# A hybrid decoder step: the meetings between head groups moved, group A's state stores and sample products spread out

## The chip, the core and the metric

The kernel runs on one core of one Trainium2 chip. The core has five engines that run their own instruction streams and meet only through semaphores: TensorE (PE, matrix products; PEld is its weight load), VectorE (DVE), ScalarE (ACT), GpSimd (POOL) and SyncE (SP, which here only issues DMA transfers). The metric is the device time of one execution in microseconds (us); lower is better.

## The reference

Two layers of a decoder trunk. Each layer normalises its input, projects it with `w_in`, runs four head groups side by side, gates and concatenates them, and projects back with `w_out`. There are 512 prompt tokens and 8 sample sequences of 4 new tokens each. The change touches group A, retention, and what stands between the groups.

```python
h = _rmsnorm(x, g)
p = _split_cols(jnp.einsum('nld,dc->nlc', h, w_in))
ret_o, ret_s = _retention(...)        # A
sb_o = _stick_breaking(...)           # B
dsa_o = _dsa(...)                     # C
rw_o, wkv_s = _rwkv7(...)             # D
x = x + jnp.einsum('nlc,cd->nld', mix, w_out)

def step(S, inp):                     # retention, one chunk
    qc, kc, vc = inp
    att = jnp.einsum('nqhd,nkhd->nhqk', qc, kc) * dmask[None]
    o = (jnp.einsum('nhqk,nkhe->nqhe', att, vc)
         + jnp.einsum('nqhd,nhde->nqhe', qc, S) * q_dec[None, :, :, None])
    S = S * s_dec[None, :, None, None] + jnp.einsum('nkhd,nkhe->nhde', kc * k_dec[None, :, :, None], vc)
    return S, o
```

For the samples each of the 8 sequences has its own state S per head (4 heads, 64 x 128). The new states are results and have to be stored (`p_ret` for the prompt, `s_ret` for the samples).

## The kernel before, in words

**The stream.** In each layer the projection by `w_in` is the bulk of the work. It is cut in 62 tiles of 128 output columns; a tile in 4 pieces (a piece is 128 x 4 x 128 weights, one DMA of 256 KB issued by SP at L336), a piece in 4 units. A unit is 6 matrix products of 128 x 272 (L319). Each piece is cast by ACT (L345, `in_w_hi`), its rest is made by DVE (L349, `in_w_lo`), and PE may use it then. Four parted pieces and three raw ones fit on the chip: the load of piece u waits until piece u-3 is parted, the cast of u until PE is done with u-4.

**The mixers beside it.** The four head groups (classes Retention, StickBreaking, Sparse, TokenMix, here A to D) run beside the stream on the same engines. Each has one generator per engine. The generator for PE says after each of its steps how many units of the stream come next (`yield 4` is four units, some 3 us). Each such yield is a mark. `Beside.follow` runs the generators of the other engines in step with those marks: at each mark they do their piece of the mixer, and then what the stream needs of them at that point. `yield n` on those engines passes n marks over; `yield LAST` passes all that are left. The four mixers start at stream unit 64, 320, 576 and 864; between the end of one and the start of the next PE runs the stream alone.

**The meetings.** The mixers share the four banks `bank`, the buffers and some semaphores, so no engine may begin the next mixer before all five have ended the last. Before, this is `meet`, called as the last thing in each of the 20 generators:

```python
def meet(engine, left, n):
    engine.drain().then_inc(left, 1)
    engine.wait_ge(left, 5 * n)
```

The engine waits until its own work is done, counts up the semaphore `left`, and waits until all five have done so.

**Group A's end.** For the samples PE computes scores (L1129), the products with the values (L1136), and then, for 4 heads and 8 sequences, the product of the old state with the 4 query columns of that sequence (L1139: 32 products, weights 128 x 128, 4 columns moving). A product in f32 is shown by the profile as two records, so L1139 has 64 records in each layer. Only heads 2j and 2j+1 share a weight `state_s[:, s, j, :]` (they lie in the upper and lower 64 rows; `qdz` holds the queries with the other half zero). Then PE gives 4 units, and for each head it makes the growth of the sample states (L1150), which DVE adds (L1259, semaphore `advanced`), with 4 units between. Norm sums (L1160) and a `yield 3` close the group.

SP loads the old states at A's start, and passes over all marks of A. After the last one it does this:

```python
yield LAST
sp.wait_ge(self.carried, QB)      # then 4 stores p_ret, 32 KB each
sp.wait_ge(self.advanced, 4)      # then 4 stores s_ret, 256 KB each
store.wait()
meet(sp, self.left, 1)
```

A stage (one layer's projection with the four mixers) ends with a barrier over all engines of its own (L142, L145).

## Time and profile before

| what | value |
|---|---|
| median of the runs | 3130.25 us |
| lowest and highest of 3 runs | 3114.84 and 3135.64 us |
| span of the profiled execution | 3141.4 us |
| mean granted TensorE clock in it | 0.945 of full |
| PE busy | 2842.2 us (90%) |
| PEld busy | 2665.1 us (85%) |
| DVE busy | 1489.0 us (47%) |
| ACT busy | 914.1 us (29%) |
| POOL busy | 110.2 us (4%) |
| share of the 16 DMA engines taken by the main queue | 31.2% |

The busy times come from one profiled execution. Lines such as L319 are lines of the kernel before. The profile's timeline lists instructions in order of their start, merged where several of one kind follow each other; in it a bracket at the end gives the idle time ahead and who ended it. The profile of a stretch gives the busy time of each engine in it, the granted clock of TensorE as a share of 2.4 GHz, and what the DMA engines did.

### The profile page before, as it was taken

Reading aid. Unit: us, or ns where it says so; the run is one execution under the profiler, and the core shown is the slowest. Engines: PE = TensorE matmul, PEld = TensorE weight load, DVE = VectorE, ACT = ScalarE, POOL = GpSimd, SP = SyncE. Lnnn points to the kernel's source line nnn. Section 1 sums busy time; section 2 is a strip of 40 time slices with the busy share of each in tenths; the row PEclk is TensorE's granted clock in tenths of the full one; section 3 lists DMA queues with packets and bytes.
Section 4 is the critical chain, followed back from the end, with each engine's and each line's share of the span. In section 5 each row is a group of like instructions: output and inputs, shape, how many; then the busy total and the mean of one; then the engine's idle time right before and its main releaser. Section 6 shows DMA issues by size and latency. Waiting matters only on the chain. (4 is left out here: it accounts for less than half of the span.)

```text
span 3141.4 us, 62551 instructions
## 1 busy us (share of the span) xinstructions
PE 2842.2 (90%) x25896; PEld 2665.1 (85%) x25896; DVE 1489.0 (47%) x2600; ACT 914.1 (29%) x1740; POOL 110.2 (4%) x155
## 2 busy tenths in 40 slices
PE   5998999999896898889979989999989959888998
PEld 5998989997785887879979989899977759788997
DVE  5322352225744485973343324421377245769533
ACT  3212252123221253232232224421332214422322
POOL 2100000000000000000001000100000000000001
PEclk7999999999998799989989999999999969999999
DMA  5323324532233122024333133354322422210443
GB/s 175 98 55 79 106 73 138 148 97 72 51 96 101 48 73 93 3 90 134 111 80 88 48 93 93 81 169 131 80 65 59 125 54 62 81 62 3 143 135 130
DMA packets 416914, 284.37 MB, mean 91 GB/s; under 512 B 44701, under 2 KB 386765, under 8 KB 413039
## 3 DMA queue, kind: packets, MB, share of 16 engines
q1 hardware_dynamic: 415710, 269.80, 31.2%
q10 hardware_dynamic: 912, 10.50, 0.9%
q8 instruction: 206, 3.38, 0.5%
q14 instruction: 86, 0.70, 0.1%
HBM read 244.04 MB, written 36.18 MB: 89 GB/s over the span
## 5 line engine op out<-in xcount | busy, mean ns | idle before, releaser
L319 PE MATMUL acc<-h_hi,in_w_hi 128*128 128x272 f32 x3968 | 900.8, 309 | 61.7 <-DVE h_lo L651 35.2
L319 PE MATMUL acc<-h_hi,in_w_lo 128*128 128x272 f32 x3968 | 833.7, 292 | 0.0
L319 PE MATMUL acc<-h_lo,in_w_hi 128*128 128x272 f32 x3968 | 833.6, 292 | 0.0
L319 PEld LDWEIGHTS acc<-h_hi,in_w_hi 128*128 128x128 f32 x3968 | 639.9, 193 | 125.6 <-issue 49.2
L319 PEld LDWEIGHTS acc<-h_lo,in_w_hi 128*128 128x128 f32 x3968 | 638.0, 193 | 0.0
L319 PEld LDWEIGHTS acc<-h_hi,in_w_lo 128*128 128x128 f32 x3968 | 634.6, 193 | 0.0
L349 DVE TENSOR_TENSOR in_w_lo<-in_w_raw,in_w_hi 128x512 fp32r<-128x512 f32 x496 | 349.1, 710 | 509.9 <-ACT in_w_hi L345 507.2
L345 ACT CAST in_w_hi<-in_w_raw 128x512 fp32r<-128x512 f32 x496 | 303.3, 617 | 506.3 <-PE acc L319 369.1
L319 PE MATMUL dr_bank<-over_both,out_weights 128*128 128x272 f32 x1984 | 280.2, 288 | 1.2 <-DVE over_both L690 1.2
L319 PEld LDWEIGHTS dr_bank<-over_both,out_weights 128*128 128x128 f32 x1984 | 260.8, 188 | 1.5 <-DVE over_both L690 1.5
L319 PE MATMUL dr_bank<-out_tiles,out_weights 128*128 128x272 f32 x1088 | 172.3, 294 | 3.8 <-DVE out_tiles L690 3.8
L349 DVE TENSOR_TENSOR out_weights<-regions,out_weights 128x512 fp32r<-128x512 f32 x128 | 88.2, 692 | 181.5 <-ACT out_weights L345 181.5
L319 PEld LDWEIGHTS dr_bank<-out_tiles,out_weights 128*128 128x128 f32 x1088 | 152.8, 194 | 4.3 <-DVE out_tiles L690 4.2
L345 ACT CAST out_weights<-regions 128x512 fp32r<-128x512 f32 x128 | 78.9, 619 | 257.1 <-PE dr_bank L319 228.9
L1574 DVE COPY region<-bank 128x512 f32<-128x512 f32 x32 | 22.1, 691 | 106.9 <-PE bank L1413 106.9
L2458 PE MATMUL dr_bank<-dr_b 64*64 64x64 f32 x1792 | 64.7, 219 | 7.1 <-DVE dr_b L2780 4.9
L2458 PEld LDWEIGHTS dr_bank<-dr_b 64*64 64x64 f32 x1792 | 59.1, 135 | 11.3 <-issue 9.3
L1910 DVE SCALAR_TENSOR_TENSOR region<-regions,region 128x128 f32<-128x128 f32 (+3 forms) x56 | 30.8, 551 | 75.3 <-ACT regions L1834 75.3
L1806 PE MATMUL bank<-table,scratch 128*128 128x128 f32 x8 | 2.2, 434 | 68.1 <-DVE scratch L1992 68.1
L1834 ACT ACTIVATE regions<-bank 128x128 f32<-128x128 f32 (+3 forms) x64 | 28.1, 439 | 120.7 <-PE bank L1725 120.7
L1420 PEld LDWEIGHTS bank<-regions,region 128*128 128x128 f32 x512 | 62.2, 192 | 0.0
L1420 PE MATMUL bank<-regions,region 128*128 128x4 f32 x512 | 61.0, 243 | 0.0
(396 smaller groups left out, 3427.9 us busy)
## 6 DMA issues: line engine op xcount, KB each, us to landing
in_w_raw<-in_w_in SPq DMA_DIRECT2D x488, 256.0 KB, 2.9
region<-in_cache_sb_kv SPq DMA_DIRECT2D x128, 256.0 KB, 3.1
regions<-in_w_out SPq DMA_DIRECT2D x128, 256.0 KB, 2.8
regions<-in_cache_dsa SPq DMA_DIRECT2D x64, 160.0 KB, 2.2
region<-x_spill SPq DMA_DIRECT2D x32, 272.0 KB, 3.4
x_spill<-region SPq DMA_DIRECT2D x32, 272.0 KB, 2.1
mix_spill<-mix SPq DMA_DIRECT2D x6, 1088.0 KB, 5.4
mix_back<-mix_spill SPq DMA_DIRECT2D x6, 1088.0 KB, 8.7
```

The source lines that it names most:

```text
L319: last = pe.matmul(self.place(i)[:, c, 0:HALF_N], w[:, u % RING, t, :], part[f][:, HALF_N * c:HALF_N * c + HALF_N], start=first and w is k ...
L345: act.copy(self.k.w_hi[:, u % RING, :, :], self.k.raw[:, u % RAW, :, :]).then_inc(self.rounded, 1)
L349: dve.tensor_tensor(self.k.w_lo[:, u % RING, :, :], self.k.raw[:, u % RAW, :, :], self.k.w_hi[:, u % RING, :, :], ALU.subtract).then_inc(s ...
L1420: last = pe.matmul(bank[:, 2, col:col + DS], self.keys[:, (u - 1) % 4, h, :], ft[:, h, NP + DS * s:NP + DS * s + DS], start=True, stop=True)
L1574: dve.tensor_copy(self.keys[:, u % 4, :, :], bank[:, u % 2, :].rearrange("p (h t) -> p h t", h=4)).then_inc(self.copied_v, 1)
L1806: pe.transpose(bank[:, 0, P * g:P * g + P], self.logit[:, P * g:P * g + P], k.c("ident"))
L1834: act.activation(self.rel[:, u % 2, 0:w], bank[:, 0, 0:w], ACT.Relu, scale=0.125).then_inc(self.rectified, 1)
L1910: last = dve.scalar_tensor_tensor(s, self.rel[:, u % 2, 0:w], g, s, ALU.mult, ALU.add)
L2458: last = pe.matmul(half(bank, r)[:, n, 4 * C * q + C * j:4 * C * q + C * j + C], left(q, j, r), right(q, j, r), start=True, stop=True)
```

## The change

Five edits; the results are the same.

1. `meet` is split. `leave` (drain, count up) stands where `meet` stood, and `arrive` (wait until the five have left) is the first line of each generator of mixers B, C and D. Nobody waits after D for the others but in the stage's own barrier.
2. SP's stores of group A are dealt over marks: a `p_ret` store at each of four marks, then an `s_ret` store at each of four more.
3. PE's 32 sample products become 16, each with 8 moving columns (4 for each of two heads).
4. PE gives 2 units after the first 8 of them and 2 after the other 8, where it gave 4 after all.
5. That makes one mark more, so ACT and DVE have one `yield` more in front of what they do with the products.

```diff
-def meet(engine, left, n):
+def leave(engine, left):
     engine.drain().then_inc(left, 1)
+
+
+def arrive(engine, left, n):
     engine.wait_ge(left, 5 * n)
...
-        for h in range(4):
+        out = bank[:, 1, 0:4 * NS].rearrange("p (h t) -> p h t", h=4)
+        for j in range(2):
             for s in range(NB):
-                last = pe.matmul(bank[:, 1, NS * h + DS * s:NS * h + DS * s + DS], self.state_s[:, s, h // 2, :],
-                                 self.qdz[:, h % 2, h // 2, DS * s:DS * s + DS], start=False, stop=(s == NB - 1), skip_group_check=True)
-        last.then_inc(self.made, 1)
-        yield 4
+                last = pe.matmul(out[:, 2 * j:2 * j + 2, DS * s:DS * s + DS], self.state_s[:, s, j, :],
+                                 self.qdz[:, :, j, DS * s:DS * s + DS], start=False, stop=(s == NB - 1), skip_group_check=True)
+            if j == 1:
+                last.then_inc(self.made, 1)
+            yield 2
...
-        meet(pe, self.left, 1)
+        leave(pe, self.left)
...
-        yield LAST
-        sp.wait_ge(self.carried, QB)
+        yield 4 + 3 + TT + 1 + 2 * QB
         for h in range(4):
             r, j = h % 2, h // 2
+            yield
+            sp.wait_ge(self.carried, QB)
             store(k.p_ret[bass.ds(l, 1), 0, h].rearrange("a d e -> (a d) e"), self.state[64 * r:64 * r + 64, j, r, :])
-        sp.wait_ge(self.advanced, 4)
         for h in range(4):
+            yield
+            sp.wait_ge(self.advanced, h + 1)
             store(k.s_ret[bass.ds(l, 1), :, h].rearrange("a s d e -> (a d) s e"), self.state_s[64 * (h % 2):64 * (h % 2) + 64, :, h // 2, :])
+        yield LAST
         store.wait()
-        meet(sp, self.left, 1)
+        leave(sp, self.left)
...
     def pe(self, pe):
+        arrive(pe, self.left, 1)
         k, ft, bank, kv = self.k, self.ft, self.bank, self.kv
```

**PE at A's sample products, before** (L1136 products with the values, L1139 the state products, L319 the stream; in these rows one row is one product, `front_4` counts the parted pieces):

```order
L1136 MATMUL bank<-regions_2,region 128x32 x3
L1139 MATMUL bank<-regions_2 128x4 x32
L319 MATMUL acc<-h_hi,in_w_hi 128x272 x2
L319 MATMUL acc<-h_lo,in_w_hi 128x272 x2
L319 MATMUL acc<-h_hi,in_w_lo 128x272 x2
L319 MATMUL acc<-h_hi,in_w_hi 128x272 x2
L319 MATMUL acc<-h_lo,in_w_hi 128x272 x2
L319 MATMUL acc<-h_hi,in_w_lo 128x272 x2
L319 MATMUL acc<-h_hi,in_w_hi 128x272 [waits front_4]
```

The same place after the change (the lines are those of the changed kernel: L1139 is the old L1136, L1143 the state products):

```order
L1139 MATMUL bank<-regions_2,region 128x32 x3
L1143 MATMUL bank<-regions_2 128x2x4 x8
L319 MATMUL acc<-h_hi,in_w_hi 128x272 x2
L319 MATMUL acc<-h_lo,in_w_hi 128x272 x2
L319 MATMUL acc<-h_hi,in_w_lo 128x272 x2
L319 MATMUL acc<-h_hi,in_w_hi 128x272 x2
L319 MATMUL acc<-h_lo,in_w_hi 128x272 x2
L319 MATMUL acc<-h_hi,in_w_lo 128x272 x2
L1143 MATMUL bank<-regions_2 128x2x4 x8
L319 MATMUL acc<-h_hi,in_w_hi 128x272 [waits front_4]
```

The one row of 32 narrow products has become two rows of 8, with two units of the stream between them.

**SP at A's end, before** (`front_33` is `carried`, `front_37` is `advanced`, `front_35` counts landed stores, `front_18` is `left`; an ISA row is the register work ahead of a DMA):

```order
L336 DMA in_w_raw<-in_w_in 128x4x128
L176 ISA [waits front_33]
L176 DMA out_p_ret<-regions_2 64x128
...
L176 DMA out_s_ret<-regions_2 64x8x128 [waits front_37]
L176 DMA out_s_ret<-regions_2 64x8x128
L176 ISA
L176 DMA out_s_ret<-regions_2 64x8x128
L176 ISA
L176 DMA out_s_ret<-regions_2 64x8x128
L336 ISA [waits front_35,front_4,front_18]
```

The same engine after the change, from the last `p_ret` store on:

```order
L176 DMA out_p_ret<-regions_2 64x128
L336 ISA [waits front_4]
L336 DMA in_w_raw<-in_w_in 128x4x128
L176 DMA out_s_ret<-regions_2 64x8x128 [waits front_37]
L336 ISA [waits front_4]
L336 DMA in_w_raw<-in_w_in 128x4x128
L176 DMA out_s_ret<-regions_2 64x8x128 [waits front_37]
L336 ISA [waits front_4]
L336 DMA in_w_raw<-in_w_in 128x4x128
L176 ISA [waits front_37]
L176 DMA out_s_ret<-regions_2 64x8x128
```

Each store now has a load of the stream behind it, and three more loads stand between the last store and the wait for the stores (`front_35`).

**PE at the meeting of A, before, and at B's first product after the change** (L1371 of the changed kernel turns a tile of B; `front_6` and `front_7` count evicted tiles):

```order
L319 MATMUL acc<-h_hi,in_w_lo 128x272 x2
L319 MATMUL acc<-h_hi,in_w_hi 128x272 [waits front_18]
L319 MATMUL acc<-h_hi,in_w_hi 128x272
L319 MATMUL acc<-h_lo,in_w_hi 128x272 x2
```

```order
L319 MATMUL acc<-h_lo,in_w_hi 128x272 x2
L319 MATMUL acc<-h_hi,in_w_lo 128x272 x2
L1371 MATMUL bank<-table,regions_2 128x128 [waits front_7,front_6,front_18]
L1371 MATMUL bank<-table,regions_2 128x128 x3
```

The wait for `left` has gone from a product of the stream to the first product of the next mixer, some 320 rows later in PE's order.

## Rows read from the trace of the kernel before

**Rows 1.** PE's waits: engine, waiting line, releaser: us in total, times, longest.

```profile
PE acc L319 <- SPq L504: 16.5, 2, 8.3
```

**Rows 2.** PE's timeline at A's meeting, both layers: start, us, line, tile, count.

```profile
272.64 0.41 PE L319 MATMUL acc<-h_lo,in_w_hi 128*128 128x272 f32 x2
272.89 0.41 PE L319 MATMUL acc<-h_hi,in_w_lo 128*128 128x272 f32 x2
281.53 0.82 PE L319 MATMUL acc<-h_hi,in_w_hi 128*128 128x272 f32 x2 [8.24 <-SPq L504]
...
285.24 0.41 PE L319 MATMUL acc<-h_hi,in_w_lo 128*128 128x272 f32 x2
...
1812.90 0.41 PE L319 MATMUL acc<-h_hi,in_w_lo 128*128 128x272 f32 x2
1821.60 0.82 PE L319 MATMUL acc<-h_hi,in_w_hi 128*128 128x272 f32 x2 [8.30 <-SPq L504]
...
1824.75 0.42 PE L319 MATMUL acc<-h_lo,in_w_hi 128*128 128x272 f32 x2
```

**Rows 3.** SP's timeline at A's meeting in layer 0 (same columns).

```profile
275.03 3.50 SPq L176 DMA_DIRECT2D out_s_ret<-regions  x4
283.14 16.75 SPq L336 DMA_DIRECT2D in_w_raw<-in_w_in  x6
```

**Rows 4.** PE's timeline in layer 0: the first product of B.

```profile
358.44 0.63 PE L1360 MATMUL bank<-table,regions 128*128 128x128 f32 x4 [0.62 <-DVE regions L380]
```

**Rows 5.** PE's timeline at B's meeting in layer 0.

```profile
657.95 0.41 PE L319 MATMUL acc<-h_hi,in_w_lo 128*128 128x272 f32 x2
658.44 0.52 PE L319 MATMUL acc<-h_hi,in_w_hi 128*128 128x272 f32 x2
```

**Rows 6.** PE's timeline at A's sample products, both layers.

```profile
221.73 1.07 PE L1136 MATMUL bank<-regions,region 32*128 32x32 f32 x8
222.73 9.88 PE L1139 MATMUL bank<-regions 128*128 128x4 f32 x64
...
237.83 1.98 PE L1150 MATMUL bank<-regions,region 32*128 32x512 f32 x4
...
1760.10 1.07 PE L1136 MATMUL bank<-regions,region 32*128 32x32 f32 x8
1761.10 12.04 PE L1139 MATMUL bank<-regions 128*128 128x4 f32 x64
...
1777.86 1.98 PE L1150 MATMUL bank<-regions,region 32*128 32x512 f32 x4
```

**Rows 7.** PE's timeline, the four units between two growth products of A.

```profile
239.74 0.52 PE L319 MATMUL acc<-h_hi,in_w_hi 128*128 128x272 f32 x2
...
242.96 1.98 PE L1150 MATMUL bank<-regions,region 32*128 32x512 f32 x4
```

**Rows 8.** Stretches within L1139: length, busy (records) by engine, clock, DMA share, GB/s.

```profile
227.00:228.00 1.00, 1.00 (x8) 1.00 (x7) 0.00 (x0) 0.00 (x0) 0.00 (x0) 0.54 0.00 0
1763.00:1764.00 1.00, 1.00 (x7) 1.00 (x7) 0.00 (x0) 0.00 (x0) 0.00 (x0) 0.54 0.00 0
```

**Rows 9.** PE's timeline at B's sample products (L1446), one of its groups.

```profile
620.28 1.84 PE L1446 MATMUL bank<-region 128*128 128x4 f32 x16
621.99 0.50 PE L319 MATMUL acc<-h_hi,in_w_hi 128*128 128x272 f32 x2
```

**Rows 10.** A stretch of B's sample products (columns as in rows 8).

```profile
620.00:624.00 4.00, 4.00 (x36) 4.00 (x35) 1.13 (x2) 0.91 (x2) 0.00 (x0) 1.00 0.57 154
```

**Rows 11.** The `s_ret` stores: time from issue to landing.

```profile
DMA to landing us min/median/max: 3.2/3.8/4.1
```

**Rows 12.** SP's timeline: a load of the stream in A's last third.

```profile
258.90 0.37 SPq L336 DMA_DIRECT2D in_w_raw<-in_w_in  x1
```

**Rows 13.** The loads of the stream from 238 to 265 us: issue to landing.

```profile
DMA to landing us min/median/max: 2.7/2.8/2.9
```

**Rows 14.** ACT's timeline: the cast of that load's piece.

```profile
266.97 0.60 ACT L345 CAST in_w_hi<-in_w_raw 128x512 fp32r<-128x512 f32 x1
```

More of the change, by code:

```diff
@@ L1198, in act @@
         yield
-        meet(act, self.left, 1)
+        leave(act, self.left)
     def dve(self, dve):
@@ L1451, in pe @@
         yield 2
-        meet(pe, self.left, 2)
+        leave(pe, self.left)
     def act(self, act):
+        arrive(act, self.left, 1)
         k, bank = self.k, self.bank
@@ L1599, in dve @@
         yield LAST
-        meet(dve, self.left, 2)
+        leave(dve, self.left)
     def pool(self, pool):
+        arrive(pool, self.left, 1)
         k = self.k
@@ L1610, in pool @@
             last.then_inc(self.own, 1)
-        meet(pool, self.left, 2)
+        leave(pool, self.left)
         yield
     def sp(self, sp):
+        arrive(sp, self.left, 1)
         k, l = self.k, self.l
@@ L1649, in sp @@
         yield
-        meet(sp, self.left, 2)
+        leave(sp, self.left)
 RING_P = 2 * PAGES
@@ L1818, in pe @@
             yield 1
-        meet(pe, self.left, 3)
+        leave(pe, self.left)
     def act(self, act):
+        arrive(act, self.left, 2)
         k, ft, bank = self.k, self.ft, self.bank
@@ L1997, in dve @@
         yield LAST
-        meet(dve, self.left, 3)
+        leave(dve, self.left)
     def pool(self, pool):
+        arrive(pool, self.left, 2)
         k, ft = self.k, self.ft
@@ L2159, in pe @@
             yield 7
-        meet(pe, self.left, 4)
+        leave(pe, self.left)
     def act(self, act):
+        arrive(act, self.left, 3)
         k, ft, bank = self.k, self.ft, self.bank
@@ L2205, in act @@
         yield LAST
-        meet(act, self.left, 4)
+        leave(act, self.left)
     def dve(self, dve):
+        arrive(dve, self.left, 3)
         k, ft, bank = self.k, self.ft, self.bank
@@ L2343, in pool @@
     def pool(self, pool):
-        meet(pool, self.left, 4)
+        arrive(pool, self.left, 3)
+        leave(pool, self.left)
         yield
     def sp(self, sp):
+        arrive(sp, self.left, 3)
         k, l = self.k, self.l
```

23 lines of the change are left out of this document (15 added, 8 removed).

## The prediction

> **What bounds the kernel now.** I read the page first: PE is busy 90% of the span, no other engine half of it, so a microsecond counts where PE stands still or where its products take longer than they need. The list of PE's waits comes next. One entry in it names a queue: PE waits 16.5 us in two pieces for SP's line of the meetings [rows 1]. The reader is to see that a DMA queue that computes nothing holds the busiest engine. The timeline shows where: at the end of group A in both layers. PE's stream stops at 272.89 us and goes on at 281.53, and stops at 1812.90 and goes on at 1821.60 [rows 2]. What SP does meanwhile stands in its own timeline: the state stores, issued only after A's last mark [rows 3], of which an `s_ret` store takes 3.8 us to land [rows 11], and SP waits for the last before it counts itself off.
>
> Third comes the granted clock, by stretches, where PE is busy and yet slow. In L1139, the sample products with 4 moving columns, PE is busy all the time, and yet the clock falls from 2.4 to 1.2 GHz within the line in both layers [rows 8].
>
> **The change part by part.**
>
> *The meeting of A.* A pair of stream products starts every 0.25 us at the full clock (272.64 to 272.89, [rows 2]). Without a stop the row at 281.53 would start at 273.14: 8.39 us lost; in layer 1 1821.60 less 1813.15, 8.45 us. Not all of it comes back, because `leave` keeps the drain. What a drain alone costs PE is seen at B's meeting, where nobody else is late: 657.95 to 658.44 is 0.49 us instead of 0.25, so 0.24 us [rows 5]. That leaves 8.15 and 8.21 us.
>
> After the stop PE runs at 1.2 GHz. In layer 0 nine pairs take from 281.53 to 285.24, 3.71 us, where nine at 0.25 take 2.25: 1.46 us; in layer 1 seven pairs take 3.15 instead of 1.75: 1.40 us [rows 2]. About 0.1 us of each belongs to the restart after a drain, so 1.35 and 1.30 us. The sum for both layers is 8.15 + 8.21 + 1.35 + 1.30 = 19.0 us.
>
> *Where the stall goes.* The wait for `left` now stands in front of B's first product. B starts on PE at 358.4 us [rows 4], 85 us after PE's last product ahead of the old meeting. SP's whole tail took until 281.5, so the last engine to leave is long through. The meetings after B and C cost PE the drain alone, which stays, so I cost them at nothing; the one after D has the stage's barrier behind it, which waits for the same engines, nothing too.
>
> *The stores dealt over marks.* The eight DMAs and their issue times are the same (3.50 us for the four `s_ret`, [rows 3]); they now stand between loads of the stream on SP. Behind each of SP's waits (`carried`, `advanced`) is queued a load of the stream, for which ACT waits, then DVE, then PE. DVE counts `advanced` up two marks before SP asks for it, and SP has by then waited for DVE's work of the mark between, so these waits cost nothing. What a store can cost is the delay of the load behind it on the DMA engines: at most its landing, 3.8 us [rows 11]. The cover is this: a load issued at 258.90 [rows 12] lands 2.8 us later [rows 13], at 261.7, and is cast only at 266.97 [rows 14]: 5.3 us of slack. One store fits; a delay over 5.3 us would reach PE. I take nothing. SP's wait for the last store now stands three loads later, some 9 us, when a store of 3.8 us has landed.
>
> *The sample products.* From the start of L1136 to the first L1150 PE took 237.83 - 221.73 = 16.10 us in layer 0, and 1777.86 - 1760.10 = 17.76 us in layer 1 [rows 6]. After the change this block holds: L1136, 1.0 us (221.73 to 222.73); twice 8 products, that is 16 records each; and twice two units. Units: four of them with their transitions took 242.96 - 239.74 = 3.22 us [rows 7], that is 12 pairs at 0.25 and 0.22 on top; two take 1.5 + 0.22 = 1.72 us. Records: the trace has no product with 8 moving columns of this kind. The nearest row is B's L1446 with 4 columns and the same weights: 16 records from 620.28 to 621.99, 1.71 us, 0.107 us each at the full clock [rows 9, 10]. As the upper end I take L1139 at a clock that was low for most of it, 12.04 / 64 = 0.188 us [rows 6]. I take 0.107, since L1446 is the same load of weights at the clock I expect, and say why I expect it just below. The block is then 1.0 + 2 x 1.71 + 2 x 1.72 = 7.9 us. The gain is 8.2 us in layer 0 and 9.9 in layer 1, together 18.1 us. With the upper end the records cost 2 x 32 x 0.081 = 5.2 us more.
>
> The Trainium skill (TensorE: Matmul & The Clock Gate, LDWEIGHTS) prices a load of weights by its columns alone, P / 1.2 ns, and so 107 ns for 128 of them, whatever moves behind it. By that page 64 records would come to an estimate of 6.8 us, the same as the sum above; that the row of 4 columns shows 0.107 agrees.
>
> *Whether the clock stays up.* L1446 is the model: 16 narrow records, then three units, over and over, and the granted clock stays at 1.00 [rows 10]. The new block has 16 records and two units, and 1.0 us of L1136 ahead. It is thinner than L1446's pattern and much denser than 64 in a row, at whose start the clock held for about 4 us in layer 0 and only 2 us in layer 1 (227 and 1763, [rows 6, 8]).
>
> The Trainium skill (same page, What's actually happening) has it that the clock falls after an idle stretch and that activity keeps it up. The rows say otherwise for narrow products: PE was busy 1.00 of the stretch when the clock fell [rows 8]. By the page the new block is safe; by the rows it is not certain.
>
> *The extra `yield` on ACT and DVE* moves their steps with the mark they belong to, nothing.
>
> **The sum.** 19.0 + 18.1 = 37.1 us. The profiled execution would go from 3141.4 to 3104.3 us. It lies 11.1 us above the median of the runs, 3130.25; on the median I forecast 3130.25 - 37.1 = 3093 us. Nothing later takes the gain back: PE is the engine that leads through B, C and D, and their starts are counted in stream units, so they move as a whole.
>
> **The rivals.**
>
> *The clock falls in the new sample block.* For it: rows 8, and layer 1 where 2 us of narrow records behind L1136 were enough. Against it: rows 10. If the second half runs at 1.2 GHz, 16 records cost 16 x 0.081 = 1.3 us more, and twelve pairs of the stream 12 x 0.2 = 2.4 us more (0.45 us a pair after the stop, [rows 2]): 3.7 us a layer. One layer gives 3097 us, both 3100 us. Chance 0.33.
>
> *The stall goes only elsewhere.* Some engine leaves late, so that PE stops at B's begin, or the stores still hold something up. Then only the sample products count: 3130.25 - 18.1 = 3112 us. For it: `arrive` waits for the same five. Against it: the 85 us. Chance 0.04.
>
> *Slower: the stores push the loads of the stream past their slack.* The place is SP's queue during A's last eight marks. It decides from a delay of 5.3 us per load on. If the slack were gone altogether and each store held PE for its landing, the four `s_ret` would cost 4 x 3.8 and the four small ones at most as much, 30 us a layer, 60 us in all; with 37 us gained, 3154 us. Against it: one store is 3.8 us and there is one per mark. Chance 0.02.
>
> *All as computed:* chance 0.61.
>
> **How the numbers follow.** The likeliest is 3093 us. The three runs of before lie between 3114.84 and 3135.64, so a median of such runs can be off by some 8 us, and the base with it. The low end takes the sum with that luck twice, 3077. The high end takes both layers at the low clock, 3100, or the dearer records, 3098, and 8 us: 3109. Between them I put 8 in 10. A measurement of this kernel can tell about 1% from no change, 31 us, so faster by over 1% means below 3099. The sum clears that by 6 us only, the clock rival by 2 in one layer and not in both, and the stall rival does not. From 0.61 of the likeliest I count 0.51 and from 0.33 of the clock 0.14 as beyond 1%: 0.65. Slower by over 1% would need the fourth case, 0.02. The rest, 0.33, is within 1%.
>
> **What would show each step.** In the changed profile PE's waits must have no entry for the line of `leave` or `arrive` of more than 0.5 us, and the stream should run on through the end of A with a step of 0.49 us at the drain. SP's `s_ret` stores should stand singly between loads, and ACT's waits for `in_w_raw` should not grow in A. From the line with the values to the first growth product PE should take 7.9 us in both layers, with the clock at 1.00; 11 to 12 us with a clock of 0.5 shows the clock rival, and 10.5 us with a clock of 1.00 shows dear 8-column products. B's first product should start some 18 us earlier in layer 0. I am wrong if PE waits at B's begin, if a load in A lands after its cast was due, or if PE loses in B, C or D what it gained here.

## The result, and the profile after

The changed kernel takes 3105.54 us in the median (3092.99 to 3117.9, 5 runs); the kernel before took 3130.81 us beside it (5 runs). The ratio is 0.9935, 95% interval 0.991 to 0.9961. So it is faster by 0.65% or 20 us by the ratio, and by 25.3 us (0.8%) in the medians, where 37.1 us were forecast. The median is inside the predicted range, and the gain inside 1%, where I had put 0.33 of the chance. In a second series the same kernel took 3100.76 us beside 3131.03 (ratio 0.9904, 0.987 to 0.9939). Of all executions in this document one was in a slower state, a run of `before_b_entry` at 3184.31 us; it is in none of the figures below.

The profiled execution has a span of 3116.1 us and a mean granted clock of 0.944. The heads of the page show the same work as before: PE 91% busy, no other engine near it.

```profile
span 3116.1 us, 62425 instructions
PE 2834.3 (91%) x25832; PEld 2656.9 (85%) x25832; DVE 1488.2 (48%) x2600; ACT 914.1 (29%) x1740; POOL 109.8 (4%) x155
```

**A did what was forecast.** In the list of PE's waits (engine, waiting line, releaser: us in total, times, longest) the entry of [rows 1] is gone, and no line of `leave` or `arrive` stands anywhere in it. The list begins with entries that have nothing to do with a meeting:

```profile
PE bank L1822 <- DVE scratch L2010: 68.5, 2, 34.5
PE acc L319 <- DVE h_lo L654: 34.9, 6, 17.1
PE bank L1766 <- ACT region L1872: 33.6, 14, 5.1
```

PE's timeline at the end of A in layer 0 (start, us, line, tile, count) answers to [rows 2]. The stream goes on; the step at the drain is 265.73 to 266.22, 0.49 us, where it was 8.64:

```profile
265.73 0.41 PE L319 MATMUL acc<-h_hi,in_w_lo 128*128 128x272 f32 x2
266.22 0.51 PE L319 MATMUL acc<-h_hi,in_w_hi 128*128 128x272 f32 x2
266.57 0.41 PE L319 MATMUL acc<-h_lo,in_w_hi 128*128 128x272 f32 x2
```

The sample block, which answers to [rows 6] (L1139 is the old L1136, L1143 the old L1139, L1155 the old L1150):

```profile
222.94 1.07 PE L1139 MATMUL bank<-regions,region 32*128 32x32 f32 x8
223.95 1.95 PE L1143 MATMUL bank<-regions 128*128 128x8 f32 x16
225.75 0.50 PE L319 MATMUL acc<-h_hi,in_w_hi 128*128 128x272 f32 x2
...
227.35 1.85 PE L1143 MATMUL bank<-regions 128*128 128x8 f32 x16
229.05 0.50 PE L319 MATMUL acc<-h_hi,in_w_hi 128*128 128x272 f32 x2
...
230.72 1.98 PE L1155 MATMUL bank<-regions,region 32*128 32x512 f32 x4
```

From 222.94 to 230.72 are 7.78 us, where the sum had 7.9; layer 1 shows the same 7.78. Sixteen records of 8 columns take 1.80 and 1.70 us from start to start, 0.106 to 0.113 us each, as the rows of 4 columns had it. The clock stays up in both layers (length, busy and records by engine, granted clock, DMA share, GB/s), which answers to [rows 8]:

```profile
223.00:231.00 8.00, 8.00 (x66) 7.81 (x66) 0.69 (x1) 0.78 (x2) 0.00 (x0) 1.00 0.28 70
1752.00:1760.00 8.00, 8.00 (x64) 7.58 (x64) 0.69 (x1) 0.78 (x2) 0.00 (x0) 1.00 0.26 69
```

From the first product with the values to B's first product PE takes 118.4 us in each layer of this profile, and took 136.7 and 138.1 us in that of before: 38.0 us less in the two layers together, where the sum had 37.1.

SP's timeline in A, answering to [rows 3]: each `s_ret` store stands between two loads of the stream. From 222 to 275 us PE has no wait at all, and ACT none for a load.

```profile
240.50 0.39 SPq L336 DMA_DIRECT2D in_w_raw<-in_w_in  x1
241.00 0.65 SPq L176 DMA_DIRECT2D out_s_ret<-regions  x1
245.00 0.39 SPq L336 DMA_DIRECT2D in_w_raw<-in_w_in  x1
```

**B gave part of it back.** B's narrow products are its v products (8 records of 32 columns) and, right behind, its page products (16 records of 4 columns, then three units of the stream, over and over; L1438 and L1446 before, L1449 and L1457 now). They begin 17.2 us earlier than before in layer 0 (573.70 where it was 590.86), and then go slower. PE's timeline, after:

```profile
573.70 1.07 PE L1449 MATMUL bank<-region 32*128 32x32 f32 x8
574.70 2.31 PE L1457 MATMUL bank<-region 128*128 128x4 f32 x16
576.88 0.80 PE L319 MATMUL acc<-h_hi,in_w_hi 128*128 128x272 f32 x2
577.48 0.66 PE L319 MATMUL acc<-h_lo,in_w_hi 128*128 128x272 f32 x2
577.93 0.65 PE L319 MATMUL acc<-h_hi,in_w_lo 128*128 128x272 f32 x2
```

and the same place of the kernel before:

```profile
590.86 1.07 PE L1438 MATMUL bank<-region 32*128 32x32 f32 x8
591.86 1.95 PE L1446 MATMUL bank<-region 128*128 128x4 f32 x16
593.67 0.50 PE L319 MATMUL acc<-h_hi,in_w_hi 128*128 128x272 f32 x2
594.01 0.41 PE L319 MATMUL acc<-h_lo,in_w_hi 128*128 128x272 f32 x2
```

A pair of the stream takes 0.45 us instead of 0.25: the clock has fallen to its lower level within the first 16 records of page products, with PE busy all the time. The stretches from the first v product to the last page product, after (first and fourth row), and those of C's products on the cached rows (L1831; the other two):

```profile
573.70:646.49 72.79, 72.79 (x535) 72.75 (x534) 9.64 (x15) 8.29 (x15) 0.00 (x0) 0.86 0.46 137
1027.14:1047.56 20.42, 20.42 (x107) 20.42 (x106) 1.83 (x3) 1.52 (x3) 0.00 (x0) 0.57 0.15 38
...
2102.47:2167.37 64.90, 64.90 (x535) 64.86 (x534) 9.63 (x15) 8.28 (x15) 0.00 (x0) 0.97 0.54 154
2547.77:2570.75 22.98, 22.98 (x107) 22.98 (x106) 1.83 (x3) 1.52 (x3) 0.00 (x0) 0.50 0.12 32
```

and before:

```profile
590.86:654.25 63.39, 63.39 (x535) 63.35 (x534) 9.63 (x15) 8.29 (x15) 0.00 (x0) 1.00 0.55 158
1034.66:1057.64 22.98, 22.98 (x106) 22.98 (x106) 1.82 (x3) 1.52 (x3) 0.00 (x0) 0.50 0.13 32
2130.42:2193.81 63.39, 63.39 (x534) 63.35 (x534) 9.63 (x15) 8.29 (x15) 0.00 (x0) 1.00 0.54 158
2574.74:2597.72 22.98, 22.98 (x106) 22.98 (x106) 1.82 (x3) 1.52 (x3) 0.00 (x0) 0.50 0.12 32
```

The same records took 9.4 us more in B of layer 0 and 1.5 in layer 1. C's block was wholly or mostly at 1.2 GHz in both profiles, but need not be: in the second profile of the changed kernel it takes 12.31 us.

```profile
576.28:639.67 63.39, 63.39 (x534) 63.35 (x534) 9.62 (x15) 8.28 (x15) 0.00 (x0) 1.00 0.55 158
1019.01:1031.32 12.31, 12.31 (x106) 12.31 (x106) 1.83 (x3) 1.52 (x3) 0.00 (x0) 1.00 0.27 63
2084.17:2153.80 69.63, 69.63 (x535) 69.59 (x534) 9.63 (x15) 8.29 (x15) 0.00 (x0) 0.90 0.51 144
2536.88:2549.24 12.36, 12.36 (x107) 12.36 (x106) 1.83 (x3) 1.52 (x3) 0.00 (x0) 0.99 0.22 58
```

So two questions for the experiments: does B's loss come with the change or from one execution to the next, and do B, and A's own block, make up all that is missing?

### The profile page after: what moved, and what is told of

Same layout as the page of the kernel before. It is cut to its first block and busy times, and to the rows that moved or that the text cites. A ratio compares the mean times of both kernels' runs of the same rounds, so it can differ in the third digit from the quotient of the medians.

```text
span 3116.1 us, 62425 instructions
## 1 busy us (share of the span) xinstructions
PE 2834.3 (91%) x25832; PEld 2656.9 (85%) x25832; DVE 1488.2 (48%) x2600; ACT 914.1 (29%) x1740; POOL 109.8 (4%) x155
## 5 line engine op out<-in xcount | busy, mean ns | idle before, releaser
L319 PE MATMUL acc<-h_hi,in_w_hi 128*128 128x272 f32 x3968 | 903.0, 310 | 43.6 <-DVE h_lo L654 34.9
L319 PE MATMUL acc<-h_lo,in_w_hi 128*128 128x272 f32 x3968 | 835.6, 293 | 0.0
L319 PE MATMUL acc<-h_hi,in_w_lo 128*128 128x272 f32 x3968 | 835.0, 293 | 0.0
L319 PEld LDWEIGHTS acc<-h_hi,in_w_hi 128*128 128x128 f32 x3968 | 641.4, 194 | 107.2 <-issue 50.1
L319 PEld LDWEIGHTS acc<-h_lo,in_w_hi 128*128 128x128 f32 x3968 | 639.7, 193 | 0.0
L319 PEld LDWEIGHTS acc<-h_hi,in_w_lo 128*128 128x128 f32 x3968 | 637.0, 193 | 0.0
L319 PE MATMUL dr_bank<-over_both,out_weights 128*128 128x272 f32 x1984 | 280.3, 289 | 1.0 <-DVE over_both L693 0.9
L319 PEld LDWEIGHTS dr_bank<-over_both,out_weights 128*128 128x128 f32 x1984 | 260.8, 189 | 1.2 <-DVE over_both L693 1.2
L319 PE MATMUL dr_bank<-out_tiles,out_weights 128*128 128x272 f32 x1088 | 172.0, 294 | 2.0 <-DVE out_tiles L693 2.0
L319 PEld LDWEIGHTS dr_bank<-out_tiles,out_weights 128*128 128x128 f32 x1088 | 152.4, 193 | 2.7 <-DVE out_tiles L693 2.6
L1457 PEld LDWEIGHTS bank<-region 128*128 128x128 f32 x512 | 64.1, 203 | 0.1
L1457 PE MATMUL bank<-region 128*128 128x4 f32 x512 | 63.0, 255 | 0.0
```

The source lines that it names most:

```text
L319: last = pe.matmul(self.place(i)[:, c, 0:HALF_N], w[:, u % RING, t, :], part[f][:, HALF_N * c:HALF_N * c + HALF_N], start=first and w is k ...
L1457: last = pe.matmul(bank[:, 3, col:col + DS], self.pages[:, w % RING_P, P * h:P * h + P], self.logs_s[:, p, col:col + DS], start=False, sto ...
```

## The experiments

### First series: both kernels again, and each half of the change alone

Four kernels on one chip, with the kernel before at 3131.03 us (29 runs). `before_again` and `after_again` have no edit. `meet_only` takes edits 1 and 2:

```diff
-        meet(pe, self.left, 1)
+        leave(pe, self.left)
...
     def pe(self, pe):
+        arrive(pe, self.left, 1)
...
-        yield LAST
+        yield 4 + 3 + TT + 1 + 2 * QB
```

`prod_only` takes edits 3 to 5:

```diff
-        for h in range(4):
+        out = bank[:, 1, 0:4 * NS].rearrange("p (h t) -> p h t", h=4)
+        for j in range(2):
...
-        yield 4
+            yield 2
```

> The kernel before, unchanged, once more. Theory 1 (the granted clock elsewhere is drawn anew in each execution): ratio 1.00 within 0.3%, but the profiled execution places its low-clock stretches otherwise than the first profile did; the stretch of B's sample products (line 1446), all at the full clock in the first profile, may show 7 to 20 us at the half clock in a layer, and the spans of its runs differ by up to 20 us with the mean granted clock between 0.944 and 0.955. Theory 2 (the change makes B's products fall to the low clock): line 1446 at the full clock in both layers again. Under both, A's stall of 8.4 us and the low clock in line 1139 are there in both layers.

> The changed kernel once more. Theory 1: ratio 0.990 to 0.995 again, and the low-clock stretch of 20 us in B's sample products of layer 0 is not where it was in the first profile: absent, or in the other layer, or shorter. Theory 2: the same 20 us in layer 0 again. Theory 3 (the gains in A were smaller in the ordinary executions): A's sample block takes clearly more than 7.8 us in at least one layer. From the first profile: A saves 18 to 20 us a layer, so with equal luck elsewhere the ratio would be 0.988.

> Only the split of the meetings and the dealt stores; A's sample products are as before (32 with 4 columns, 4 units behind). Sum of the prediction: 19.0 us less, ratio 0.994. PE must not stop at A's end, and SP's stores stand singly between the loads. Theory 1: 0.992 to 0.996, whatever the clock elsewhere. Theory 2 in the form that the shift of the work against the clock costs the rest: ratio nearer 1.00 than 0.994.

> Only A's sample products changed (16 with 8 columns, two units behind each 8, and the extra yields on ScalarE and VectorE); the meetings and the stores are as before. Sum of the prediction: 18.1 us less, ratio 0.994. The block takes 7.8 us in both layers at the full clock, and the stall of 8.4 us at A's end stays. Theory 1: 0.992 to 0.996. If a low clock in the sample block were avoided only to come up a little later (the stall follows 30 us behind it), the ratio would be 0.996 or more.

| kernel | median us (runs) | ratio to before, 95% | span of its profile |
|---|---|---|---|
| before_again | 3119.67 (12) | 0.9983 (0.9957 to 1.001) | 3117.3 |
| after_again | 3100.76 (6) | 0.9904 (0.987 to 0.9939) | 3090.9 |
| meet_only | 3124.51 (12) | 0.9971 (0.9944 to 0.9998) | 3122.0 |
| prod_only | 3124.21 (12) | 0.998 (0.9957 to 1.0004) | 3126.4 |

By the medians each half alone is worth 6.5 and 6.8 us (by the ratios 9 and 6) of the 19.0 and 18.1 that the sum gave it, though their rows in A are as computed: `meet_only` has no stop at the meeting, and `prod_only`'s block takes 11.5 and 9.3 us instead of 16.1 and 17.8. In `meet_only` B's stretch takes 71.2 and 68.0 us where 63.4 is the hot one. So the time goes behind A. Theory 3, a smaller gain in A itself, has no row for it. But single executions of one kernel differ by 30 us, and `before_again`, which has no edit at all, came out 11.4 us below the kernel before in the median. Two profiles of before and of the changed kernel and one of each half can't tell a drawn clock from a moved one. What was needed was a kernel in which B and C don't fall.

### Second series: opening the entries

The begin of a mixer's narrow products is its entry. I call it closed where two kinds of narrow products stand back to back (in C, one unit between its groups) and opened where more units of the stream stand between. A block is hot when its clock is 2.4 GHz throughout.

The kernel before took 3126.64 us here (29 runs). `after_b_entry` puts two units between B's v products and its first page products, and moves SP's part by one mark:

```diff
                       start=(h == 0), stop=False, skip_group_check=True)
+        yield 2
         for u in range(NB * PAGES):
...
-        yield 2
+        yield 3
```

> The changed kernel, and in it two units of other work between B's v products and its first page products, so that the narrow products of the two kinds do not stand back to back (about 1 us and 1.7 us of them in the rows of after). Nothing is left out. Theory P (the gain of A goes back into B because B's narrow products now meet the clock where it falls: its block took 71.8 and 63.9 us with 20.5 and 3.4 us at 0.50, against 62.4 us without a low stretch): with the entry opened, B's block shows no low stretch in either layer and takes 62.4 us, so the kernel gains the mean of what B loses in the profiles of after, (9.4 + 1.5) / 2 to (9.4 + 6.2) / 2 = 5 to 8 us a layer, 10 to 15 us in all: about 3093 where after gives 3103, a ratio to before of 0.985 to 0.99. Theory R (low stretches fall anywhere and are drawn anew in each execution): B's block still shows low stretches of 3 to 20 us, and the time is after's, ratio 0.993. Theory S (A's own gain is smaller in ordinary executions): also after's time.

`before_b_entry` is the same edit on the kernel before.

> The kernel before with that one edit in B alone: two units between B's v products and its first page products. Nothing is left out. Theory P: B's block was hot already in the profiles of before (62.4 us in both layers of one, 62.4 and 63.9 us in the other), so there is nothing to gain: ratio 0.997 to 1.001. If the same edit gives as much here as it gives in the changed kernel (10 us or more, 0.996 or less), B's losses are none of the change's doing, and theory P falls.

`before_shift` adds 8 narrow products at the begin of B's part of PE, in the kernel before:

```diff
         self.stream.tile_kept(pe, 19)
+        for _ in range(8):
+            pe.matmul(bank[:, 3, 0:DS], k.c("ident"), k.c("ident")[:, 0:DS], start=True, stop=True)
```

> The kernel before, and 8 narrow products (4 columns of the constant identity on itself, into a place that is overwritten) added at the begin of B's part of PE in each layer. Their result is used nowhere. Their own price, from the rows of after (0.107 us a record, 2 records a product): 16 x 0.107 = 1.7 us, in both layers 3.4 us at most, that is a ratio of 1.001 at most. Theory P (what matters is where B's narrow products stand in time after A's): a displacement of B by so little changes B's low stretches, and the block takes 64 to 72 us in place of 62.4: 3 to 19 us more, ratio 1.002 to 1.007. Theory R: nothing beyond the 3.4 us, and B's block at 62.4 us as often as in before.

`three_blocks` opens A's, B's and C's entries in the changed kernel (and moves ACT's, DVE's and SP's marks by one in A). In A:

```diff
                       start=(h == 0), stop=False, skip_group_check=True)
+        yield 2
         out = bank[:, 1, 0:4 * NS].rearrange("p (h t) -> p h t", h=4)
```

and in C:

```diff
         pe.transpose(bank[0:NS, 1, 0:P], self.logit[:, PAST:PAST + NS], k.c("ident")).then_inc(self.turned_p, 1)
-        yield 2
+        yield 3
...
                 last.then_inc(self.applied_p, 1)
-            yield 1
+            yield 2
```

> The changed kernel with the entry of all three narrow blocks opened: two units between A's value products and its first state products, two between B's v products and its first page products, and in C two units instead of one between the groups of products on the cached rows and three instead of two behind its transpose. Nothing is left out. Theory P: A's block keeps 7.8 us and B's 62.4 us, with no low stretch, and C's block (23.0 us with the clock at 0.50 throughout, 12.3 us with it at 1.00, in the profiles so far 6 times slow or nearly so of 12) is always at 12.3 us plus its units: 10.7 us x 2 layers x one half = 11 us more than the entry of B alone gives, about 3082, ratio 0.982 to 0.987. Theory R: low stretches move elsewhere, ratio 0.99 to 0.993.

| kernel | median us (lowest to highest, runs) | ratio to before, 95% |
|---|---|---|
| after_b_entry | 3099.05 (3085.68 to 3126.72, 12) | 0.9917 (0.9886 to 0.9947) |
| before_b_entry | 3139.65 (3123.29 to 3144.78, 11) | 1.0028 (1.0003 to 1.0053) |
| before_shift | 3133.67 (3122.36 to 3147.85, 12) | 1.0023 (0.9997 to 1.0049) |
| three_blocks | 3083.27 (3080.45 to 3086.58, 5) | 0.9864 (0.9826 to 0.9901) |

Opening the entry works on the clock: B's stretch is 64.9 us (63.4 and 1.5 for the two units) with the clock at 1.00 in both layers of `after_b_entry`, of `before_b_entry` and of `three_blocks` (and in every later profile with this entry, 18 layers in all). But `after_b_entry` as a whole is not told from the changed kernel (0.9917 against 0.9935 and 0.9904): C's block, 12.3 us in one layer and 20.7 in the other here, scatters by more than B's loss. `before_shift` missed theory P's forecast: B's stretch stayed at 63.4 us in both layers, and its 7 us over before are not told from the 3.4 of the added records. `before_b_entry` came out slower, which no theory had; its B is hot, one of its C blocks was at the low clock (20.5 us), and why its median lies 13 us above before (9 by the ratio) I can't say.

`three_blocks` met its forecast, 1.4% faster than before, and it brought the quiet that was wanted: its runs lie within 6 us, those of before within 33. The entry of B in a quiet kernel (from `three_again`, the same program, below) looks like this; the first page products stand behind two units and keep their 0.107 us a record:

```profile
574.13 1.07 PE L1450 MATMUL bank<-region 32*128 32x32 f32 x8
575.13 0.52 PE L319 MATMUL acc<-h_hi,in_w_hi 128*128 128x272 f32 x2
...
576.74 1.84 PE L1459 MATMUL bank<-region 128*128 128x4 f32 x16
578.44 0.50 PE L319 MATMUL acc<-h_hi,in_w_hi 128*128 128x272 f32 x2
```

### Third series: the sum of A on quiet ground

The kernel before took 3127.22 us (21 runs). `three_again` is `three_blocks`. `hot_before` is the kernel before with B's and C's entries opened, as shown, and nothing of the change; `hot_meet` is `meet_only` with the same; `three_no_b` is `three_blocks` without B's two edits:

```diff
                       start=(h == 0), stop=False, skip_group_check=True)
-        yield 2
         for u in range(NB * PAGES):
```

> The kernel of three_blocks once more, as the base of the three others here. Nothing is left out. Its A block was 7.8 us plus a unit, its B block 62.3 us and its C block 17.5 us with the units in it, each with the clock at 1.00 throughout in both layers, and its five runs lay within 6.2 us (3080.5 to 3086.6) where the runs of before spread over 33. Expected again: 3083, ratio 0.984 to 0.987, spread under 15 us.

> The kernel before (its stop at A's meeting, its stores held back and its 16 column sample products as they were), with the entries of B and C opened as in three_blocks, so that no narrow block behind A can fall. Nothing is left out. Theory Q (the sum for A was right, and the missing 13 us went into blocks behind it): with B and C unable to fall, the whole A gain stands: from the last state product's line to the begin of B's first stage PE takes 139.2 and 140.7 us in before (142.8 and 142.0 in its second profile) and 121.2 in three_blocks, 20.0 us a layer, so hot_before should be 37 to 40 us over three_again: about 3121, and its own spread under 20 us. Theory S (A's gain is smaller in ordinary executions): 25 to 30 us over three_again, about 3110.

> meet_only (the engines meet at the next mixer's begin, the stores dealt over marks, A's sample products still 16 columns wide), with the entries of B and C opened as in three_blocks. Nothing is left out. Theory Q: the meeting's share of the sum was 19.0 us, the sample products' 18.1, each of them full once B and C cannot fall: hot_meet is 18 to 20 us over three_again and 19 us under hot_before, about 3102. In the open field meet_only gained only 5 to 6 us of its 19 (3119.5 against 3125.0 in mean span). Theory S: hot_meet is within 10 us of hot_before.

> three_blocks with B's entry as the changed kernel has it (v products and first page products back to back), and A's and C's opened. Nothing is left out. Theory P: B's block falls in a good half of the executions, 71.8, 63.9, 62.4, 68.6, 70.2 and 67.0 us in the six layers profiled with the new meeting against 62.4, so a mean of 4.9 us a layer: 8 to 12 us over three_again, about 3093, single runs between 3081 and 3105, and B's block with a low stretch in at least one layer of the profile. Theory R: as three_again, within 3 us and with its small spread.

| kernel | median us (lowest to highest, runs) | ratio to before, 95% |
|---|---|---|
| three_again | 3078.16 (3076.97 to 3083.72, 6) | 0.9854 (0.9814 to 0.9893) |
| hot_before | 3116.09 (3108.47 to 3123.12, 12) | 0.9963 (0.9938 to 0.9988) |
| hot_meet | 3100.18 (3095.99 to 3105.6, 10) | 0.9921 (0.9895 to 0.9947) |
| three_no_b | 3085.35 (3078.56 to 3094.51, 6) | 0.9872 (0.983 to 0.9913) |

With B and C unable to fall the change to A is worth 3116.09 - 3078.16 = 37.9 us, and the sum was 37.1. The runs of the two do not overlap; by the two ratios to before it would be 34 us, so I read it as 34 to 38. Theory S (a smaller gain in A) had 25 to 30 and falls. The meeting's share is 3116.09 - 3100.18 = 15.9 us (19.0 forecast), that of the products 3100.18 - 3078.16 = 22.0 (18.1).

Closing B's entry again costs 3085.35 - 3078.16 = 7.2 us (the runs of the two overlap), a little under the 8 to 12 expected, and the profile shows it in the place named. `three_no_b`, B's stretches in both layers:

```profile
574.16:639.11 64.95, 64.95 (x534) 64.91 (x534) 9.62 (x15) 8.28 (x15) 0.00 (x0) 0.97 0.53 154
2079.83:2149.46 69.63, 69.63 (x535) 69.59 (x534) 9.62 (x15) 8.28 (x15) 0.00 (x0) 0.90 0.50 144
```

and `three_again`, B's and C's (with their added units):

```profile
574.13:639.02 64.89, 64.89 (x547) 64.85 (x546) 9.64 (x15) 8.29 (x15) 0.00 (x0) 1.00 0.54 155
1018.39:1035.96 17.57, 17.57 (x149) 17.57 (x148) 2.90 (x5) 2.45 (x5) 0.00 (x0) 1.00 0.22 57
```

### Fourth series: does B's closed entry cost the kernel before anything?

The kernel before took 3128.96 us (15 runs). `before_c`, `meet_c` and `after_c` are the kernel before, `meet_only` and the changed kernel with C's entry alone opened (the C diff above). `three_held` is `three_blocks` with A's stores held back as before:

```diff
-        yield 4 + 3 + TT + 1 + 2 * QB + 1
+        yield LAST
+        sp.wait_ge(self.carried, QB)
...
-            yield
-            sp.wait_ge(self.advanced, h + 1)
...
-        yield LAST
         store.wait()
```

> The kernel before with C's entry opened alone (its units as in three_blocks); B's v products and first page products stay back to back. Nothing is left out. Theory P1 (with A's old stop ahead of it B stands where its clock hardly ever falls: 63.4, 63.4, 63.4 and 64.9 us from its first v product to its last page product in the four layers profiled of before, and 63.4 twice in before_shift): B's closed entry costs nothing here, and before_c is within 3 us of hot_before, about 3116. Theory P2 (B's entry falls as often with the old meeting as with the new): 7 us over hot_before, about 3123.

> meet_only with C's entry opened alone; B's is closed, A's sample products are 16 columns wide. Nothing is left out. Theory P1: without the stop at A's meeting B's clock falls (71.2 and 68.0 us in meet_only's profile, where 63.4 is the hot block), so 6 to 12 us over hot_meet's 3100.2: 3106 to 3112, and a low stretch in B in at least one layer of the profile. Theory P2: 7 us over hot_meet too, 3107, but then before_c is at 3123. If meet_c is within 3 us of hot_meet, the new meeting doesn't matter for B.

> The changed kernel with C's entry opened alone: B's and A's stay closed. Nothing is left out. Theory P: as three_no_b (3085.4), and A's own closed entry adds what its falls cost, 1.5 and 7.9 us in two of the six layers profiled (9.3 / 6 x 2 = 3 us an execution): about 3088, range 3083 to 3094. If it is at 3085 or less, A's entry costs nothing.

> three_again with A's state stores held back until all else of the mixer is out, as in the kernel before, while the engines still meet at the next mixer's begin. Nothing is left out. The prediction put the dealing of the stores at no cost, and left open what it is worth. If holding them back delays B's loads (SP waits for the last states and then for the stores' landing, 3.8 us, before the next mixer's part begins; the slack read of the first load was 5.3 us): 0 to 4 us a layer, 3078 to 3087. If SP's place at the meeting hides it all: 3078 as three_again.

| kernel | median us (lowest to highest, runs) | ratio to before, 95% |
|---|---|---|
| before_c | 3116.9 (3108.72 to 3120.01, 10) | 0.9971 (0.9952 to 0.9991) |
| meet_c | 3100.98 (3099.04 to 3110.74, 6) | 0.9914 (0.9893 to 0.9936) |
| after_c | 3094.27 (3090.19 to 3099.05, 5) | 0.9888 (0.9865 to 0.991) |
| three_held | 3083.47 (3081.67 to 3091.77, 5) | 0.9859 (0.9836 to 0.9882) |

In the old surroundings B's closed entry costs nothing: `before_c` is where `hot_before` was (0.9971 and 0.9963), and B's stretch is 63.39 us in both layers. With all of the change it does: `after_c`, at the upper edge of its forecast (3083 to 3094), lies 22.6 us under `before_c`, not 37.9. Its B in layer 0:

```profile
574.40:647.17 72.77, 72.77 (x535) 72.73 (x534) 9.62 (x15) 8.28 (x15) 0.00 (x0) 0.86 0.48 138
2090.31:2153.70 63.39, 63.39 (x535) 63.35 (x534) 9.63 (x15) 8.28 (x15) 0.00 (x0) 1.00 0.55 158
```

`meet_c` missed its forecast of 6 to 12 us over `hot_meet`: 0.8 us, on another chip, with B at 64.9 and 63.4 us. So the meeting alone doesn't move B onto the falling clock on the whole, though it did in `meet_only`'s one profile; the losses are sure only where meeting and products are both changed. `three_held` against `three_blocks` and `three_again` (0.9859 against 0.9864 and 0.9854): whether the stores are dealt or held back makes no difference that can be seen, once the wait stands at B's begin. The intervals are too wide for the 0 to 4 us a layer in question, but the rows say the same: from A's sums of squares (L1166) to B's first product PE takes 89.0 us in both layers of `three_held` and of `three_blocks`.

### Last series: A's own entry

The kernel before took 3123.47 us (7 runs). `three_no_a` is `three_base` (again `three_blocks`) without the two units at A's entry:

```diff
-        yield 2
         out = bank[:, 1, 0:4 * NS].rearrange("p (h t) -> p h t", h=4)
```

> three_blocks with A's entry as the changed kernel has it (value products and first state products back to back), B's and C's opened. Nothing is left out. If A's closed entry is the rest of the missing 15.3 us, it is 8 us over three_base; if only its falls as profiled count (9.3 us and 1.5 us in the eight layers of the changed A block, so 2.7 us an execution), it is 2 to 4 us over; if it costs nothing, 0, and then 8 us of the difference lie between the chips or in neither entry alone.

> three_blocks once more, as the base of three_no_a on the same chip. Nothing is left out. Its medians were 3083.3 and 3078.2 on two chips; again 3078 to 3084.

`three_base` took 3083.62 us (3075.69 to 3088.0, 4 runs; ratio 0.9861, 0.983 to 0.9892), `three_no_a` 3084.58 us (3081.11 to 3088.3, 4 runs; 0.9869, 0.9839 to 0.9899): 1.0 us. In its profile A's block fell for 3.4 us in one layer, which cost 1.5 us. So A's closed entry is hardly 8 us, though four runs on either side that spread over 7 and 12 us can't rule it out by themselves.

## Why the prediction was wrong

**The stop at A's meeting, 19.0 us: right in its place, near in size.** The wait is gone, no engine's `left` holds PE at B's begin, and on quiet ground it is 15.9 us. From A's first product of L1160, its sums of squares (L1163 in `hot_meet`), to B's first product PE takes 100.1 and 100.2 us in `hot_before`'s profile and 90.5 twice in `hot_meet`'s, 19.3 us in all; from the start to A in layer 0 and from C's end there to A in layer 1, where nothing of A was changed, PE took 7 us more in `hot_meet`'s profile, with more of that time at the low clock. One reading in the sum was off: from 281.53 to 285.24 us stand eight pairs and not nine, so the slow restart in layer 0 cost 1.6 us and not 1.35, and the term should have been 19.3.

**The drain that stays, 0.24 us: right.** The step is 0.49 us in both layers.

**The stall goes nowhere (rival 3112): right.** No wait for `left` shows on PE in any profile with the new meeting.

**The dealt stores, nothing (rival 3154): right**, and `three_held` adds that by its rows dealing them isn't needed either.

**The sample products, 18.1 us: right.** The block is 7.78 us for 7.9 forecast, and 8 columns cost what 4 cost. The Trainium skill (TensorE: Matmul & The Clock Gate, LDWEIGHTS) prices a load of weights by its columns alone, 107 ns for 128; at the full clock the rows agree with 0.106 to 0.113 us a record.

**The clock in the new block (rival 3097 or 3100): it exists, and costs less on the mean.** In ten layers profiled with the new block, its closed entry and the new meeting it stayed hot in six, fell for 3.4 us in three (1.5 us each) and for 17.1 us once (7.8 us): 12.3 / 10 = 1.2 us a layer and 2.5 an execution. In `prod_only`, with the old meeting, it fell in both layers, for 17.1 and for 3.4 us; with these it is 1.8 us a layer. The prediction put 3.7 on a layer that falls, and single falls lay on either side of that. `three_no_a` has the two layers together at 1.0 us. The rows of before that spoke against the rule of the Trainium skill (TensorE: Matmul & The Clock Gate, What's actually happening) were the better guide: the block is thinner in narrow records than the old one, but not safe.

**The step that failed** is the last of the sum: "Nothing later takes the gain back: PE is the engine that leads through B, C and D, and their starts are counted in stream units, so they move as a whole." It named this itself as a sign of being wrong ("if PE loses in B, C or D what it gained here"). B's start does move as a whole, and no wait takes anything back. But what a block of narrow products costs depends on the clock it meets, and B's does not meet the same one after the move. Profiled stretches of B with its closed entry (63.4 us is the hot one):

| A ahead of it | B's stretch, us, by layer | mean over 63.4 |
|---|---|---|
| old: before, before_again, before_shift, before_c | 63.4, 63.4, 63.4, 64.9, 63.4, 63.4, 63.4, 63.4 | 0.2 |
| new products alone: prod_only | 64.9, 63.4 | 0.8 |
| new meeting alone: meet_only, meet_c | 71.2, 68.0, 64.9, 63.4 | 3.5 |
| both: after, after_again, after_c, three_no_b | 72.8, 64.9, 63.4, 69.6, 72.8, 63.4, 65.0, 69.6 | 4.3 |

By these rows B gives back 2 x (4.3 - 0.2) = 8.2 us an execution, and `three_no_b` measured 7.2. With A's own 1.0 to 2.5 us that is 8 to 11 us of the 37.9, which leaves 27 to 30; the changed kernel gained 25.3 and 30.3 us in the medians of its two series (20 and 30 by the ratios). The first series lies lower than that by its ratio, but its interval is 16 us wide. So the cause is shown in the main: the sum for A is whole when B and C can't fall, and B's closed entry, free in the kernel before, costs about 7 us in the changed one.

**What stays open.** Between `before_c` and `after_c` 15.3 us of the 37.9 are missing, and the rows and runs account for 8 to 11; the rest, 4 to 7 us, lies across two chips, and one program differed by 5 us between two series (3078.16 and 3083.27). If the held stores of `three_held` cost nothing, as the rows have it, it can stand in for `three_blocks` on the chip of the fourth series. There the quiet kernels are 3116.9 - 3083.47 = 33.4 us apart, and `after_c` lies 10.8 us above `three_held`: the closed entries of A and B then account for all that is missing on that chip, and the rest is the distance between 37.9 and 33.4 from chip to chip.

One more place behind A shows in the traces and was not tested. From B's last page product to C's first product behind its transposes (L1810 of before) PE takes 377.9 and 378.1 us in `hot_before`, 379.8 and 380.1 in `hot_meet`, and 378.2 to 380.7 in the eight layers of `three_blocks`, `three_again`, `three_base` and `three_held` (379.5 on the mean), with 51 us of it at the low clock in `hot_before` and 55 to 61 in the others. So some 1.5 us a layer are given back there even on quiet ground, where every narrow block is hot; the 38.0 us between A's sample products and B's begin are the fuller measure of what A gained.

Why B is spared behind the old A is not known either. Displacing B by 16 records didn't bring the falls about (`before_shift`), nor did the new meeting alone on the whole (`meet_c`), so "B stands at an unlucky place" is argued and not shown; shown is that it fell in six of eight layers with the changed A ahead, and in one of eight with the old one.

**The base and C's block.** C's block (23.0 us at the low clock, 12.3 at the high one, and 2.5 us more behind it) was wholly or mostly at the low clock in 8 of 18 layers profiled with its entry closed: 4 of 10 with the old meeting, 4 of 8 with the new. By these layers it hardly bears on the change, but it makes most of the scatter that a range must hold: with it opened, before's 37 us between lowest and highest in that series (3112.58 to 3149.14) shrink to 15 in `hot_before`, and the median drops by 11 to 12 us. Whether C falls more often behind the new meeting the runs leave open: by the ratios, opening C alone gave `meet_only` 18 us and the kernel before 9, each within 6 to 8 us. C also differs from A and B in what stands ahead: PE waits 34 us for DVE there, at the low clock. In three of the eight low layers that clock went on through the block; in the other five it rose 0.4 to 0.8 us ahead of the block and fell again 3 us into it. The profiled execution of before had both blocks at the low clock. I had read its distance of 11.1 us to the median as luck of no consequence; it was a price with a place in the trace.

## What to carry to other kernels

When an edit displaces later work in time, list the later blocks of narrow products, and ask of each whether it can fall to the lower clock where it will stand; a sum that holds for the edited stage can lose a fifth to a block that the diff doesn't touch. Where two kinds of narrow products meet (8 records and 16 here, 2.7 us), two units of wide work between them cost 1.5 us that is only moved, and keep the clock up. With the change and all three entries opened the kernel is 1.4% faster than before, and its runs agree to 12 us or better where those of before in the same series spread over 16 to 37. And when a few microseconds are to be told apart, build the quiet version first: on it the change's 37.9 us could be read from six runs and twelve.

## What the runs showed of the hardware

TensorE's granted clock went from 2.4 to 1.2 GHz in the midst of blocks where PE was busy 1.00 of the time, at the change from 8 records of 32 columns to 16 of 4, and stayed there for 3.4 to 20.5 us while pairs of wide stream products took 0.45 us instead of 0.25. The later groups of 16 narrow records with three units between ran at 1.00 throughout in the hot stretches. The Trainium skill (TensorE: Matmul & The Clock Gate, What's actually happening) has the clock fall after idleness; no idle time stands ahead of 574.70 in the rows of after. In nine profiles of kernels without C's edit the same block of C, behind a wait of 34 us, took 12.3 us in some layers and 20.4 to 23.0 in others, with the same instructions; two executions of one program lie up to 30 us apart by such choices, and a program whose three narrow blocks are opened by a few units lay within 6.1, 6.8 and 12.3 us in its three series.
